# Norms of three layers moved behind their products, and the first v products ahead of the last mean, in a two-block transformer kernel on one Trainium2 core

## The reference, cut to what matters

```
h = rms_norm(x, norm_mix)                      # norm 0: x * rsqrt(mean(x*x) + 1e-6) * gain
proj = h @ w_in                                # q, k, v of two attentions, and two gates
x = x + merged @ w_out                         # norm 1 and the expert layer (PEER) follow
x = x + peer_ffn(rms_norm(x, norm_ffn), ...)
h = rms_norm(x, norm_ple)                      # norm 2: the sigmoid layer
x = x + sigmoid(h @ w_ple_gate) * (p @ w_ple)
# second block
proj = rms_norm(x, norm_mix_2[0]) @ ab_w_in    # norm 3: diff attention's q, k, v and the pooling's u
x = x + concat(diff_attention(q, k, v), pool_mixer(u)) @ ab_w_out
x = x + relu(rms_norm(x) @ w1)**2 @ w2         # norm 4, FFN 0
x = x + gla(rms_norm(x, norm_mix_2[1]))        # norm 5: linear attention; q, k, v, g_out, gk_low = h @ gla_w_in
x = x + relu(rms_norm(x) @ w1)**2 @ w2         # norm 6, FFN 1
return rms_norm(x, norm_final)                 # norm 7
```

## Time and profile before

| | us |
|---|---|
| runs | 3450.75, 3459.63, 3448.74; median 3450.75 |
| profiled execution, its own time | 3446.91 |
| its span, first to last instruction | 3445.1 |
| TensorE busy | 3340.8 (97%) |
| VectorE, ScalarE, POOL busy | 1605.2 (47%), 1186.7 (34%), 1330.9 (39%) |
| mean granted TensorE clock | 0.987 |

### The profile page before, as it was taken

The page is one execution under the profiler, slowest core; times in us unless marked ns, Lnnn a source line. Parts: engine busy times, 40 slices in busy tenths (PEclk is TensorE's granted clock), DMA queues, the critical chain, the costliest instruction groups (busy, mean ns, idle before and its releaser), DMA issues.

```text
span 3445.1 us, 41579 instructions
## 1 busy us (share of the span) xinstructions
PE 3340.8 (97%) x15792; PEld 2713.3 (79%) x15792; DVE 1605.2 (47%) x2908; ACT 1186.7 (34%) x1665; POOL 1330.9 (39%) x582
## 2 busy tenths in 40 slices
PE   8999998999999999999999999888999999999998
PEld 5687777888888888888888888676888878878886
DVE  6825227996454441165565554326411134652112
ACT  4444223333333333332222222335422234433231
POOL 4420233444333334344444444334444433434442
PEclk9999999999999999999999999999999999999999
DMA  3130222343545456576666664221232321122222
GB/s 118 68 123 13 92 98 76 116 145 129 198 170 191 173 183 222 160 203 186 186 191 183 189 189 130 84 92 42 93 98 92 97 91 70 41 74 94 96 92 86
DMA packets 424823, 428.09 MB, mean 124 GB/s; under 512 B 146512, under 2 KB 343760, under 8 KB 423008
## 3 DMA queue, kind: packets, MB, share of 16 engines
q1 hardware_dynamic: 424672, 426.00, 38.7%
HBM read 354.63 MB, written 69.21 MB: 123 GB/s over the span
## 4 chain that ended last, share of the span: by engine, by line
PE 77%; issue 12%; POOL 5%; DVE 3%; ACT 1%; DMA 1%; POOLq 0%; SPq 0%; DVEq 0%; PEldq 0%; ACTq 0%
PE pb L653 22%; PE pb L655 22%; PE pb L654 22%; POOL s_over L577 5%; PE pb L934 3%; PE pb L858 1%; DMA s_ring<-w 1%; PE pb L843 1%; PE pb L821 1%; PE pb L955 1%; PE pb L725 0%; DVE s_arena L1721 0%; PE pb L885 0%; PE pb L831 0%; PE pb L860 0%
## 5 line engine op out<-in xcount | busy, mean ns | idle before, releaser
L577 POOL TENSOR_TENSOR s_over<-s_ring,s_rhigh 128x1024 fp32r<-128x1024 f32 x518 | 1256.4, 2427 | 2051.3 <-ACT s_rhigh L1223 2051.1
L1223 ACT ACTIVATE s_rhigh<-s_ring 128x1024 fp32r<-128x1024 f32 x518 | 548.6, 1060 | 1417.8 <-DMA s_ring<-w 588.3
L653 PE MATMUL pb<-s_over,s_rhigh 128*128 128x512 f32 x2112 | 834.9, 395 | 0.0
L655 PE MATMUL pb<-s_over,s_over 128*128 128x512 f32 x2112 | 833.7, 395 | 0.0
L654 PE MATMUL pb<-s_over,s_rhigh 128*128 128x512 f32 x2112 | 833.7, 395 | 0.0
L653 PE MATMUL pb<-s_hS,s_rhigh 128*128 128x512 f32 (+1 forms) x1888 | 757.8, 401 | 40.8 <-DVE s_hS L1658 23.3
L655 PE MATMUL pb<-s_hS,s_over 128*128 128x512 f32 (+1 forms) x1896 | 735.0, 388 | 0.0
L654 PE MATMUL pb<-s_hS,s_rhigh 128*128 128x512 f32 (+1 forms) x1888 | 732.0, 388 | 0.0
L654 PEld LDWEIGHTS pb<-s_over,s_rhigh 128*128 128x128 f32 x2112 | 397.2, 188 | 95.2 <-issue 0.7
L653 PEld LDWEIGHTS pb<-s_over,s_rhigh 128*128 128x128 f32 x2112 | 397.2, 188 | 94.9 <-issue 0.7
L655 PEld LDWEIGHTS pb<-s_over,s_over 128*128 128x128 f32 x2112 | 397.2, 188 | 94.8
(11 more groups left out here) (261 smaller groups left out, 2711.6 us busy)
## 6 DMA issues: line engine op xcount, KB each, us to landing
s_ring<-w SPq DMA_DIRECT2D x272, 512.0 KB, 3.5
s_ring<-eu SPq DMA_DIRECT2D x128, 512.0 KB, 4.0
s_ring<-ev SPq DMA_DIRECT2D x128, 512.0 KB, 4.1
acts<-s_arena SPq DMA_DIRECT2D x128, 256.0 KB, 4.1
gates<-s_arena SPq DMA_DIRECT2D x8, 4096.0 KB, 13.9
s_arena<-acts SPq DMA_DIRECT2D x128, 256.0 KB, 4.3
s_arena<-gates SPq DMA_DIRECT2D x128, 256.0 KB, 4.4
s_xT<-xT SPq DMA_DIRECT2D x4, 512.0 KB, 7.7
```

The lines of the kernel that those rows point to most:

```text
L577: gp.tensor_tensor(rlow[:, s, :, :], ring[:, s, :, :], rhigh[:, s, :, :].bitcast(F32), ALU.subtract).then_inc(S("w_split"), 1)
L653: mm(dst, a_high, b_high, start=start, stop=False)
L655: return mm(dst, a_low, b_high, start=False, stop=stop)
L1223: sc.activation(rhigh[:, s, :, :], ring[:, s, :, :], ACT.Copy).then_inc(S("w_high"), 1)
```

## The change

Norms 2, 3 and 5 get the second form. `plain` (ScalarE) and `low_plain` (VectorE) make the parts of x * gain within the last updates of x, norm 2 and 5 into hS, norm 3 into hF. The mean stands behind the first half's products of p (norm 2) or behind the first tile (3 and 5). Results are multiplied by r: the gates on VectorE ahead of the sigmoid, q and k on VectorE in place of ScalarE's copies, v on ScalarE with a column of r, which TensorE turns behind tile 4 (`turn_root`), u and the output gates on POOL, the decay gates' low product on VectorE. pT is loaded ahead of the last 12 expert tiles, into a place of its own; the linear attention's small tables behind its tile 3 in place of tile 7; its two clears stand ahead of the reciprocal. In the first stage the row of roots is turned behind tile 17, the v products use banks 5 and 4, and the first two stand ahead of the last mean. The rest are numbers of semaphores that follow from it.

```diff
-MS_BANK = [4, 7, 3, 7, 3, 3, 7, 3]
+MS_BANK = [4, 7, 7, 7, 3, 3, 7, 3]
+        r_row = rstd[:, 0, :]
+        r_col = sb("r_col", [P, 8])
 SP
+            sp.dma_start(pT, a["pT"]).then_inc(S("p_in"), 16)
             for r in range(12):
                 n = T_V + 116 + r
...
             tiles(T_PLE, T_PLE + RING, W_PLE)
-            sp.wait_ge(S("x_upd"), X_PEER)
-            sp.dma_start(pT, a["pT"]).then_inc(S("p_in"), 16)
...
-            tiles(T_GLA, T_GLA + 8, W_GLA)
+            tiles(T_GLA, T_GLA + 4, W_GLA)
             sp.wait_ge(S("x_upd"), X_F0)
...
-            tiles(T_GLA + 8, T_GLA + 32, W_GLA + 8)
+            tiles(T_GLA + 4, T_GLA + 32, W_GLA + 4)
 POOL
                 src = du[:, gi, :]
+                gp.wait_ge(S("rstd_done"), 4)
+                gp.tensor_tensor(src, src, r_row, ALU.mult).then_inc(S("pool_a"), 1)
...
-            splits(T_F0, T_GLO + RING)
+            splits(T_F0, T_GLA + 16 + RING)
+            gp.wait_ge(S("rstd_done"), 6)
+            for n in range(DC):
+                gp.wait_ge(S("lg_copied"), n + 1)
+                gp.tensor_tensor(lg[:, n, :], lg[:, n, :], r_row, ALU.mult).then_inc(S("lg_normed"), 1)
+                splits(T_GLA + 16 + RING + n, T_GLA + 16 + RING + n + 1)
 TensorE
+            def turn_root(k):
+                pe.wait_ge(S("rstd_done"), k + 1)
+                for t in range(TT):
+                    m = mm(pb[:, 6, t:t + 1], rstd[0:1, 0, t * P:(t + 1) * P], mats[0:1, M_ID, 0:1],
+                           start=t == 0, stop=t == TT - 1)
+                m.then_inc(S("r_turned"), 1)
...
+            def value(n):
+                k, t = divmod(n, TT)
+                tile0 = (T_VD12, T_VD12 + 2, T_VA, T_VA + 2, T_VD0)[k]
+                if n >= 2:
+                    pe.wait_ge(S("v_copied"), n - 1)
+                h = hu if k < 2 else (hS[:, 0, :, :], hS[:, 1, :, :])
+                by_token(pb[:, 5 - n % 2, 0:2 * P], tile0, tokens_of(t), h).then_inc(S("v_done"), 1)
...
-            for i in range(22):
+            for i in range(21):
...
+                if i == 17:
+                    pe.wait_ge(S("rope_sin"), 12)
+                    for b in range(2 * TT):
...
+                    m.then_inc(S("r_turned"), 1)
+                if i == 20:
+                    pe.wait_ge(S("h_by_u"), 2 * DC)
+                    pe.wait_ge(S("r_copied"), 1)
+                    value(0)
+                    value(1)
                 if 1 <= i <= 20:
                     pe.wait_ge(S("qk_eps"), i)
...
-            norm(2)
             pe.wait_ge(S("p_in"), 16)
             for half in range(2):
                 w = slot(T_PLE + 5 * half)
-                if half:
-                    pe.wait_ge(S("x_upd"), X_PEER + 4)
                 for o in range(4):
+                    if half:
+                        pe.wait_ge(S("x_upd"), X_PEER + o + 1)
...
                 m.then_inc(S("tile_done"), 1)
+                if half == 0:
+                    norm(2)
                 for o in range(4):
                     if half == 1:
-                        pe.wait_ge(S("e_sig"), o + 1)
+                        pe.wait_ge(S("e_scaled"), o + 1)
...
-            norm(3)
-
+            pe.wait_ge(S("x_upd"), X_PEER + 5)
             for i in range(8):
                 if i >= 4:
-                    pe.wait_ge(S("d_copied"), i - 3)
-                linear(T_AB + i, i % 4, hwait=H_NORM[3] if i == 0 else None)
+                    pe.wait_ge(S("qk_out"), i - 3)
+                linear(T_AB + i, i % 4, h=hF, hwait=H_NORM[3] if i == 0 else None)
+                if i == 0:
+                    norm(3)
+                if i == 4:
+                    turn_root(3)
+            pe.wait_ge(S("r_copied"), 2)
...
-            norm(5)
             for i in range(8):
+                if i == 3:
+                    pe.wait_ge(S("std_done"), 6)
                 if i >= 4:
                     pe.wait_ge(S("l_copied"), i - 3)
                 linear(T_GLA + i, i % 4, hwait=H_NORM[5] if i == 0 else None)
+                if i == 0:
+                    norm(5)
+                if i == 4:
+                    turn_root(5)
+            pe.wait_ge(S("r_copied"), 3)
 ScalarE
+            def plain(k, c, x_before, dst):
+                sc.wait_ge(S("x_upd"), x_before - 7 + c)
+                sc.activation(dst[:, 0, c, :], xT[:, c, :], ACT.Identity, scale=col(C_GAIN + 8 * k + c))\
+                    .then_inc(S("h_high"), 1)
+                square(k, c, x_before)
+
+            def column(k):
+                sc.wait_ge(S("r_turned"), k + 1)
...
+                sc.activation(r_col[:, 0:TT], pb[:, 6, 0:TT], ACT.Copy).then_inc(S("r_copied"), 1)
...
             mean_root(2)
-            highs(2)
             for o in range(DC):
                 parts(T_PLE + 4 + o + (o >= 4))
-                sc.wait_ge(S("tile_done"), T_PLE + 2 + o + (o >= 4))
-                if o >= 2:
-                    sc.wait_ge(S("x_upd"), X_PEER + o - 1)
-                sc.activation(esig[:, o % 2, :], pb[:, 4 + o % 4, :], ACT.Sigmoid).then_inc(S("e_sig"), 1)
+                sc.wait_ge(S("e_scaled"), o + 1)
+                sc.activation(esig[:, o % 2, :], esig[:, o % 2, :], ACT.Sigmoid).then_inc(S("e_sig"), 1)
                 if o >= 1:
-                    square(3, o - 1, X_PLE)
-            square(3, 7, X_PLE)
+                    plain(3, o - 1, X_PLE, hF)
+            plain(3, 7, X_PLE, hF)
             mean_root(3)
-            parts(T_AB + 2)
-            highs(3)
...
+            parts(T_AB + 10)
+            column(1)
...
             mean_root(5)
-            highs(5)
...
+            parts(T_GLA + 10)
+            column(2)
 VectorE
-            ve.wait_ge(S("x_upd"), X_PEER)
-            norm(2)
+                if r >= 121:
+                    low_plain(2, r - 121, hS)
+            low_plain(2, 7, hS)
+            invert_root(2)
             for o in range(DC):
-                if o >= 2:
-                    sum_square(3, o - 1)
+                ve.wait_ge(S("tile_done"), T_PLE + 2 + o + (o >= 4))
+                ve.tensor_tensor(esig[:, o % 2, :], pb[:, 4 + o % 4, :], r_row, ALU.mult).then_inc(S("e_scaled"), 1)
                 ve.wait_ge(S("e_sig"), o + 1)
...
                 ve.tensor_tensor(xT[:, o, :], xT[:, o, :], et[:, o % 2, :], ALU.add).then_inc(S("x_upd"), 1)
-            ve.wait_ge(S("x_upd"), X_PLE)
-            norm(3)
+                if o >= 1:
+                    low_plain(3, o - 1, hF)
+                if o >= 2:
+                    sum_square(3, o - 1)
+            low_plain(3, 7, hF)
+            invert_root(3)
...
+            for i in range(8):
+                dst3 = dq[:, i, :] if i < 4 else dk[:, i - 4, :]
+                ve.wait_ge(S("tile_done"), T_AB + i + 1)
+                ve.scalar_tensor_tensor(dst3, pb[:, i % 4, :], 0.125 if i < 4 else 1.0, r_row, ALU.mult, ALU.mult)\
+                    .then_inc(S("qk_out"), 1)
...
-            ve.wait_ge(S("x_upd"), X_F0)
-            norm(5)
...
+            low_plain(5, 7, hS)
             ve.memset(latt, 0.0)
             ve.memset(lks[:, 1, :], 0.0)
+            invert_root(5)
```

More of the change, by code:

```diff
@@ L109, in raw @@
 def raw(n):
-    return n - DC * sum(h < n for h in (H_NORM[0], H_CAT, H_NORM[4]))
+    return n - DC * sum(h < n for h in (H_NORM[0], H_NORM[2], H_NORM[3], H_CAT, H_NORM[4], H_NORM[5], H_NORM[6]))
 X_MIX = 8
@@ L328, in program @@
         ga = Area(2 * 2 * 8 * T).take(2, T)
+        pT = Area(2 * 2 * 8 * T + 2 * T).take(2, T)
         C = Area()
@@ L361, in program @@
         E = Area()
-        pT = E.take(2, T)
         esig = E.take(2, T)
@@ L1413, in _ @@
                 if r >= 120:
-                    square(2, r - 120, X_PEER)
+                    plain(2, r - 120, X_PEER, hS)
             def norm_plain(k, x0, t0):
@@ L1419, in norm_plain @@
                     parts(t0 - 5 + c)
-                    sc.wait_ge(S("x_upd"), x0 - 7 + c)
-                    sc.activation(hF[:, 0, c, :], xT[:, c, :], ACT.Identity, scale=col(C_GAIN + 8 * k + c))\
-                        .then_inc(S("h_high"), 1)
-                    square(k, c, x0)
+                    plain(k, c, x0, hF)
                 mean_root(k)
@@ L1431, in hidden @@
                         if j >= 24:
-                            square(k_next, j - 24, x_next)
+                            if k_next == 5:
+                                plain(5, j - 24, x_next, hS)
+                            else:
+                                square(k_next, j - 24, x_next)
                         continue
@@ L1538, in _ @@
             mean_root(5)
-            highs(5)
-            for i in range(8):
-                parts(T_GLA + i + 3)
-                sc.wait_ge(S("tile_done"), T_GLA + i + 1)
-                dst2 = lq[:, i, :] if i < 4 else lk[:, i - 4, :]
-                sc.activation(dst2, pb[:, i % 4, :], ACT.Copy, scale=float(P ** -0.5) if i < 4 else 1.0)\
-                    .then_inc(S("l_copied"), 1)
-            sc.wait_ge(S("gk_low"), 1)
```

(7 more changed lines are left out.)

125 lines of the change are left out of this document (62 added, 63 removed).

## The result

| | before | after |
|---|---|---|
| median of the runs | 3449.74 us | 3422.62 us |
| lowest to highest | 3448.06 to 3459.63 (4) | 3421.30 to 3424.05 (4) |
| profiled execution; its span | 3446.91; 3445.1 | 3422.53; 3420.8 |

The ratio is 0.9921, with an interval of 0.9909 to 0.9934: 27.1 us faster. The forecast was 3408, 42 us faster, in a range that ended at 3423. So the direction and the order of size were right, and 15 us of the gain are missing. That the time still lies inside the range, by 0.4 us, is luck: the upper end was the price of a rival, 'POOL holds VectorE', and what took the 15 us was mostly something else.

A forecast was written before the change was run, and what follows sets the result against it. TensorE, busy for 97% of the span, was taken as the bound. 9.1 - 1.7 + 25.0 - 0.8 - 0.1 + 11.0 = 42.5 us won, so 3450.75 becomes 3408, range 3399 to 3423.

The forecast's parts named there:

- POOL holds VectorE: Rival: in the sigmoid layer and diff attention POOL's work delays VectorE; 15 us less won, 3423; chance 0.10.
- B: Sigmoid layer and norm of the diff layer: TensorE's waits go, 72.2 us against 99.5; net 25.0 us won.
- D: Norm of the linear attention: two tiles and a mean take 12.6 us against 24.5; 11.0 us won after the turn.
- C: Diff attention: POOL's four multiplications cost 0.8 us, from between 0 and 5.2, and the scaled v copies 0.1.
- the stall of 0.3 us ahead of chunk 7 of hF: First diff tile: asks for chunk 7 at T + 4.9, ready at T + 5.1 after sigmoid tile 7; stall 0.3 us.
- A: First v products: turn moved, two products ahead of the last mean; 9.1 us won, 1.7 given back to the clock.
- The v products win little: Rival: weight tile 23 lands late or the clock stays low in the first group; 5 us less, 3413; chance 0.06.
- the slower case: Clock falls at the diff layer's tiny matmuls, stays 1.2 GHz to the attention's end; 87 us, 3495; chance 0.02.
- The rival in which the norms stay on the path: Waits for the reciprocal or the column replace the old ones, tile for tile; 3445 to 3455; chance 0.02.

The follow-up runs named there:

- the runs with the copies first once and twice: Against the kernel at 3373.45: v copies ahead of rounding the next weight pair in the first stage, 3369.2 us; also in the linear attention, 3378.0 us.
- the run without D: Norm 5 with its loads, copies, gates and v copies as before, against the kernel with the column behind the arena (3413.0): 3420.4 us.

## Why the prediction was right in its direction and short by 15 us

**B and D, right.** Together with C they were to win 35.1 and won 31.7. The steps that the prediction listed can be seen: over 68 us of the sigmoid and diff layers, and over 52 behind FFN 0, TensorE doesn't pause, at the full clock:

```profile
2162.00:2230.00 68.00, 68.00 (x265) 49.47 (x264) 31.45 (x42) 30.53 (x40) 23.85 (x10) 1.00 0.24 86
```

```profile
2778.00:2830.00 52.00, 52.00 (x240) 40.15 (x239) 13.89 (x14) 10.18 (x11) 21.52 (x9) 1.00 0.27 96
```

The column, pT, the reciprocal and the scaled gates are waited for nowhere, and the turns cost 1.05 where 0.9 stood. Even the stall of 0.3 us ahead of chunk 7 of hF didn't show. D was also undone by a run; B was not, so its share is read from the stage alone. (B's own sum has a slip of no weight: 27.3 less 0.9 and 1.3 is 25.1, not 25.0.) The stage of D isn't free of the low clock: 0.97 over its 239.4 us, all of it behind the norm, after 0.95 over 248.8 before.

**The failed step: no term for the allocation.** The change part by part lists instructions, waits, loads and banks, and has no term for `r_col` itself, nor for what lies behind it. That term is -9, and it was put at nothing without a reason: 32 bytes move the arena, and 6,600 matmuls take 1.0 to 1.9 ns longer each. The runs with the column behind the arena (3413.0) and with the 32 bytes alone (+8.8) show it from both sides. The number was there to be seen: the prediction read 5.44 us for a tile with hS and 5.57 for one with hF, took the difference as a property of the arena and charged 10 tiles with 0.13 each. It didn't ask why two buffers of one memory differ by 2.4%, and so missed both that a shift could make it worse and that it could be abolished for 40 us.

**A, mis-sized.** Forecast 7.4, measured 4.4 in the medians and 5.7 in the stages, and 1.9 in the changed kernel's own profile, which has the long wait. The turn was put at 1.9 us, "half of 3.71": it took 2.9, and the clock behind it fell, 1.7 more; 4.6 in all (the mean behind linear 19 ended 5.6 us later than before, of which 0.9 stood there ahead of the turn). Why 2.9 can be read if the sixteen records are split in two, in the changed kernel and in the kernel before:

```profile
146.21 1.05 PE L755 MATMUL pb<-s_mats,s_rstd 1*128 1x1 f32 x8
147.13 2.00 PE L755 MATMUL pb<-s_mats,s_rstd 1*128 1x1 f32 x8
```

```profile
168.01 1.86 PE L745 MATMUL pb<-s_mats,s_rstd 1*128 1x1 f32 x8 [6.81 <-DVE s_arena L1687]
169.74 1.98 PE L745 MATMUL pb<-s_mats,s_rstd 1*128 1x1 f32 x8
```

The first four matmuls read 128 neighbouring roots, and at the full clock they took little more than half of their 1.86. The last four read every fourth root (`slice(b - TT, T, 4)`), and took 2.0 at either clock. So "half" held for one half of the turn. The code differs in nothing else there, but no run has the step changed alone, so that it is the step is argued, not shown.

The wait before v product 2 was put at 2.2 and is 2.00, and there the clock did not fall (1.00), where 1.7 had been charged. That charge rested on a slip: of the two cases read, 1.8 us at 1.00 and 2.7 us at 0.75, the prediction took the second as the nearer to 2.2, and the first is. The order of ScalarE that makes this wait was read rightly; that the same order, four groups later, would meet loads that are not yet there was not looked at. It gives back 1.9 us of wait (3.45 for 1.54) in this profile, and 1.7 in clock over the 10 us around it; how much of the latter belongs to the wait is open, as the kernel at 3413.0, with a wait of 1.5 there, had 0.93 over the 25 us from 220 on. For this profile that adds up: 7.4 - 1.0 - 1.7 for the turn, + 1.7 + 0.2 at v product 2, - 0.9 from the start, - 1.9 - 1.7 for the late pair, 2.1, where 1.9 was measured.

**C, mis-sized.** 0.8 was taken from between 0 and 5.2, and the whole of the multiplications is 2.0, read in the one pair of profiles.

**The rivals.** "POOL holds VectorE" gave 3423, which is what was measured, and by another road: in B, where it put most of its price, the first low part was indeed slowed (1.31 us for 0.74) and nothing waited for it. Only its part in C was real, and small. "The v products win little" is the one that came in, for 3 us of its 5, though by a turn and a late pair that it didn't name. The clock stood at 1.00 from the diff layer's turn to the attention (2253 to 2292) and at 0.97 in the attention, where it had been 0.94, so the slower case had nothing to stand on. The rival in which the norms stay on the path is out: no wait of TensorE names the column, the reciprocal or the scaled tiles.

**Added up:** 42.5 forecast; -9 for the place, -1.7 to -3 for A, -1.2 for C beyond its term, -1 for D. That leaves 28 to 30, and 27.1 was measured. What remains is of the size of a stall that no term covers and that the medians may hold: in seven of the twelve profiles of kernels with the change and in neither of the two without it, TensorE waits once, for 1.4 to 4.7 us, near 800 us, when the expert gather begins, as here in the runs with the copies first once and twice:

```profile
PE pb L945 <- DVE s_arena L1951: 1.5, 1, 1.5
```

```profile
PE pb L945 <- DVE s_arena L1951: 2.9, 1, 2.9
```

VectorE is then at the end of a long chain of choices. The changed kernel's own profile doesn't have it, the run with the first stage as before does (2.9), so an earlier start alone isn't its cause. This stays open.

## What to carry to other kernels

Before costing instructions, look at what a diff allocates, and ahead of what: a buffer of 32 bytes moved the 112 KB a partition behind it and cost a quarter of what the change had won. If two groups of the same matmul have different start-to-start distances in a trace, ask for the reason; here it was, for most of the difference, the distance of the operand from the weights within 256 bytes, and setting it to 0 won more than the change. And an order of roundings and copies that is right in one loop can be wrong in the next: it depends on whether the load or the split comes last there.

## What the runs showed of the hardware

- **The start-to-start distance of an fp32r matmul of 512 columns depends on where its moving operand stands relative to the weights.** Measured at 2.4 GHz, by how far the operand's place lies beyond the weights', modulo 256 bytes: 0 apart 0.2267 us, 64 apart 0.2289, 96 apart 0.2333, 128 apart 0.2324 to 0.2333, 160 apart 0.2343, 192 apart 0.2333. The two values at 128 occur with buffers at the same bytes (0.2333 and 0.2324 for the experts' down products, in the kernel at 3413.0 and in the run without D), so the place isn't all. Moving everything by the same amount changed nothing. At 0 the runs show a period of 512 bytes at most; that it is 256 rests on hF and the arena at 128, 160 and 192. Whether the weights or another buffer that moved with them is the other end was not told apart, nor why; no matmul spacing was found under 0.2267.
- Sixteen records of one-column matmuls in a row (2.9 us) were followed by 2.9 us at a granted clock of 0.50, 1.2 GHz, in the changed kernel; over the 9 us around them the eleven profiles that have them there show 0.62 or 0.81, and the three that have them elsewhere 1.00. Eight records (1.05 us) left it at 1.00.
- TensorE's idle time of 2.0 us ahead of v product 2 left the clock at 1.00; that of 3.45 us came with 0.83 over 10 us.
- Eight records of one-column matmuls whose weights are 128 neighbouring numbers of one row took 1.05 us at a clock of 1.00 and 1.86 at 0.50; eight whose weights are every fourth number took 2.00 and 1.98.
